# Low parts of the projection weights on VectorE in place of GpSimd, in the joined norm and projection stage of a two-block kernel

## The reference

```
for l in range(2):
    h = rmsnorm(x, mix_norm[l])                 # x: 512 x 1024
    p = h @ w_in[l]                             # w_in[l]: 1024 x IN_COLS
    qkv, z, beta_r, a_r, ... = split(p)         # qkv: 1536 columns, z: 512, beta_r and a_r: 8 each
    qkv = silu(depthwise_conv5(qkv))
    q, k, v = split(qkv)                        # 4 heads of 128 each
    q = l2norm(q) * 128 ** -0.5;  k = l2norm(k)
    beta = sigmoid(beta_r)
    g = -exp(a_log) * softplus(a_r + dt_bias)
    ... gated delta rule on q, k, v, beta, g, a second scan, the output projection, an FFN
```

## Time and profile before

| | us |
|---|---|
| median of 3 timed runs | 3571.25 (3570.12 to 3573.18) |
| the profiled execution | 3573.7 |
| its span in the trace | 3571.8 |
| POOL's busy time in the span | 320.2 |
| DVE's busy time in the span | 1649.7 |

### The profile page before, as it was taken

How to read it: one execution, slowest core, us unless ns; L and a number is a source line. 1 busy time by engine, 2 the same in 40 slices (tenths; PEclk the granted TensorE clock), 3 DMA queues, 4 the chain that set the end, 5 groups by cost and what they waited for, 6 DMA issues and landing times. The chain is left out here.

```text
span 3571.8 us, 41903 instructions
## 1 busy us (share of the span) xinstructions
PE 3124.3 (87%) x15948; PEld 2596.9 (73%) x15948; DVE 1649.7 (46%) x2194; ACT 1143.8 (32%) x1604; POOL 320.2 (9%) x228
## 2 busy tenths in 40 slices
PE   7898998987999898989998799995954689979999
PEld 5798987865887678988877588774832468758787
DVE  4566557334553365654743455333345333333233
ACT  3443643223222353354332322233102123232222
POOL 2231021001000133300200100001000000010000
PEclk9999999998999999999999899997955589989999
DMA  4101202322222310020042222223200023223222
GB/s 140 47 1 43 75 1 60 98 67 83 94 82 82 107 47 25 1 93 24 19 112 71 71 94 94 72 69 72 71 6 24 1 75 99 85 71 94 71 97 91
DMA packets 256603, 234.91 MB, mean 66 GB/s; under 512 B 22885, under 2 KB 240211, under 8 KB 255828
## 3 DMA queue, kind: packets, MB, share of 16 engines
q1 hardware_dynamic: 256468, 233.07, 21.4%
HBM read 226.75 MB, written 6.29 MB: 65 GB/s over the span
## 5 line engine op out<-in xcount | busy, mean ns | idle before, releaser
L120 PE MATMUL PS<-HHI,WHI 128*128 128x512 f32 x2080 | 825.2, 397 | 126.8 <-DVE WLO L172 112.2
L121 PE MATMUL PS<-HLO,WHI 128*128 128x512 f32 x2080 | 820.7, 395 | 0.0
L122 PE MATMUL PS<-HHI,WLO 128*128 128x512 f32 x2080 | 820.5, 394 | 0.0
L172 DVE TENSOR_TENSOR WLO<-RAW,WHI 128x1024 fp32r<-128x1024 f32 (+3 forms) x256 | 436.7, 1707 | 559.3 <-ACT WHI L168 558.2
L168 ACT CAST WHI<-RAW 128x1024 fp32r<-128x1024 f32 (+3 forms) x256 | 367.5, 1438 | 825.6 <-PE PS L122 692.0
L120 PEld LDWEIGHTS PS<-HHI,WHI 128*128 128x128 f32 x2080 | 394.7, 190 | 221.4 <-issue 82.4
L121 PEld LDWEIGHTS PS<-HLO,WHI 128*128 128x128 f32 x2080 | 394.8, 190 | 88.4 <-issue 1.0
L122 PEld LDWEIGHTS PS<-HHI,WLO 128*128 128x128 f32 x2080 | 394.2, 189 | 88.1
L120 PE MATMUL PS<-SH,WHI 128*128 128x512 f32 x800 | 317.0, 396 | 44.4 <-DVE SL L379 44.4
L121 PE MATMUL PS<-SL,WHI 128*128 128x512 f32 x800 | 315.6, 394 | 0.0
L122 PE MATMUL PS<-SH,WLO 128*128 128x512 f32 x800 | 315.2, 394 | 0.0
(11 more groups left out here) (394 smaller groups left out, 4220.5 us busy)
## 6 DMA issues: line engine op xcount, KB each, us to landing
RAW<-in_w_up SPq DMA_DIRECT2D x44, 1024.0 KB, 5.1
RAW<-in_w_in SPq DMA_DIRECT2D x68, 512.0 KB, 4.1
RAW<-in_w_in SPq DMA_DIRECT2D x27, 1024.0 KB, 5.3
RAW<-in_w_down SPq DMA_DIRECT2D x44, 512.0 KB, 3.2
RAW<-in_w_gate SPq DMA_DIRECT2D x32, 512.0 KB, 4.0
RAW<-in_w_mlp SPq DMA_DIRECT2D x16, 1024.0 KB, 5.5
RAW<-in_w_mlp SPq DMA_DIRECT2D x32, 512.0 KB, 3.2
RAW<-in_w_out SPq DMA_DIRECT2D x24, 512.0 KB, 3.4
```

What stands on the lines that cost most here:

```text
L120: e.matmul(out, wh, xh, start=first and n == 0, stop=False)
L121: e.matmul(out, wh, xl, start=False, stop=False)
L122: last = e.matmul(out, wl, xh, start=False, stop=final and n == len(quads) - 1)
L172: self.lo_st.done(dve.tensor_tensor(self.lo[:, s], self.raw[:, s], self.hi[:, s], ALU.subtract), f"unit{s}")
```

## The change

POOL's loop over tiles 4 to 15 goes. DVE gets `low(u)`, the same subtraction with the same wait for the high part, and calls it twelve times, between the convs: low(4) ahead of conv(0), low(5) behind it, low(6) behind conv(1), low(7) behind conv(2), and from conv(4) on low(i + 4) behind conv(i). The semaphore is the same under a new name. PE's, ACT's and SP's orders stay.

```diff
         def low_ready(e, u):
-            e.wait_ge(lo_dve, u + 1) if u < N else e.wait_ge(lo_pool, u - N + 1)
+            e.wait_ge(lo_dve, u + 1) if u < N else e.wait_ge(lo_late, u - N + 1)
...
+                def low(u):
+                    dve.wait_ge(hi_s, u + 1)
+                    dve.tensor_tensor(WLO[:, u % N], RAW[:, u % N], WHI[:, u % N], ALU.subtract).then_inc(lo_late, 1)
...
+                low(4)
                 conv(0)
+                low(5)
                 dve.wait_ge(S["ba_done"], 1)
                 dve.tensor_copy(BAT[0:16, :], PS[0:16, 7, :]).then_inc(S["ba_kept"], 1)
                 conv(1)
+                low(6)
                 conv(2)
+                low(7)
                 dve.wait_ge(S["ba_turned"], 1)
...
                 for i in range(3, 8):
                     conv(i)
+                    if i >= 4:
+                        low(i + 4)
                 dve.wait_ge(gate.sem, gate.place["ea"])
...
                 conv(8)
+                low(12)
...
                 conv(9)
+                low(13)
                 for n in range(4):
                     unit(n)
                 conv(10)
+                low(14)
                 for n in range(4, 8):
                     unit(n)
                 conv(11)
+                low(15)
...
             def _(pool):
                 for k in range(K):
                     pool.wait_ge(S["x_hi"], k + 1)
                     pool.tensor_tensor(pair[1][:, k, :], TK[k % 4], pair[0][:, k, :], ALU.subtract).then_inc(S["x_lo"], 1)
-                for u in range(N, T):
-                    pool.wait_ge(hi_s, u + 1)
-                    pool.tensor_tensor(WLO[:, u % N], RAW[:, u % N], WHI[:, u % N], ALU.subtract).then_inc(lo_pool, 1)
```

More of the change, by code:

```diff
@@ L427, in qkv_stage @@
     TK = [S2[:, n, :] for n in range(4)]
-    names = ("loaded0", "loaded1", "loaded2", "loaded3", "weights_hi", "weights_lo_dve", "weights_lo_pool", "tiles_done",
+    names = ("loaded0", "loaded1", "loaded2", "loaded3", "weights_hi", "weights_lo_dve", "weights_lo_late", "tiles_done",
              "wba_in", "wba_hi", "wba_lo", "eps_set", "x_squares", "x_sums", "x_root", "x_normed", "x_hi", "x_lo",
@@ L434, in qkv_stage @@
         loaded = [S[f"loaded{s}"] for s in range(N)]
-        hi_s, lo_dve, lo_pool, used = S["weights_hi"], S["weights_lo_dve"], S["weights_lo_pool"], S["tiles_done"]
+        hi_s, lo_dve, lo_late, used = S["weights_hi"], S["weights_lo_dve"], S["weights_lo_late"], S["tiles_done"]
         wl = A["w_in"][l].rearrange("(k p) n -> p k n", p=P)
```

## The result

| | before | after |
|---|---|---|
| median of 5 timed runs, us | 3573.18 (3570.12 to 3578.76) | 3600.35 (3593.70 to 3606.97) |
| the profiled execution, us | 3573.7 | 3606.97 |
| its span, us | 3571.8 | 3605.1 |
| its mean granted clock | 0.924 | 0.916 |

The change makes the kernel slower by 0.73%: the ratio is 1.0073, with a 95% interval of 1.0055 to 1.0092. That is 27 us, where 15.4 were forecast. The sign and the mechanism in the stage were right; the time lies outside the range of 3580 to 3590.5. The profiled execution of the changed kernel was the slowest of its five.

A forecast was written before the change was run, and what follows sets the result against it. PE was taken to bound the stage; per layer 5.5 us of idle plus 2.2 us of slow restart make 7.7, +15.4 us for two layers, so 3571.25 becomes 3586.6 us. The range was 3580 to 3590.5 us.

The forecast's parts named there:

- The bound and the spot: PE bounds the stage; five lows in DVE's full stretch delay Ln 0, so PE idles 5.5 us before the third sum.
- A low's price: Each subtraction moved to DVE costs 1.14 us in its queue, between 1.14 and 1.23.
- Rival D: Each low on DVE costs 1.23 us: 0.9 us more, 3587.5, inside the forecast's 76%.
- What was costed at nothing: low(4), (5) and low(11) to (15) on DVE were taken as hidden, costing PE 0.
- The slow restart: After idling before the third sum, PE restarts at the 1.2 GHz level, losing 2.2 us per layer.
- Rival A: PE idles before the third sum but its clock stays up: +11 us, 3582.3; chance 13%.
- Rival B: DVE's convs shrink without POOL's work beside them, so silu(7) stays in place: no change, 3571.3; chance 6%.
- After that nothing gives it back: Behind the third sum PE is the bound again, so its 5.5 us idle per layer is not recovered.
- two times 7.7: Both layers each lose 5.5 us of PE idle time plus 2.2 us of slow restart: +15.4 us.
- the phase of the clock is not in my hand: Remark in favour of PE's clock staying up after its idle time before the third sum; no size given.

The follow-up runs named there:

- e1: Changed kernel with low(6) to low(10) made by POOL again, the other seven lows still on DVE; 3582.84 us, ratio 1.0027.
- e2: Kernel before, all lows on POOL, plus five equal-size subtractions on DVE at the places of low(6) to low(10); 3603.35 us, ratio 1.0083.
- e11: Kernel before with 15 unused matmuls per layer added ahead of dense(15); 3583.83 us, ratio 1.0034.
- e12: Changed kernel with 15 unused matmuls per layer added ahead of dense(15); 3611.17 us, ratio 1.0101.
- e5: Changed kernel with 4 unused matmuls per layer added ahead of dense(15); 3598.66 us, ratio 1.0077.
- e8: Changed kernel with low(6) to low(10) back on POOL, plus 4 unused matmuls per layer ahead of dense(15); 3586.18 us, ratio 1.0033.
- e3: Changed kernel with dense(10) put ahead of the eight sums in PE's order; 3577.24 us, ratio 1.0009.
- e13: Changed kernel with 24 unused matmuls between the second and third sum, filling PE's wait; 3590.48 us, ratio 1.0045.
- e14: Changed kernel as it is, measured again on the same chip; 3597.18 us, ratio 1.0069.

## Why the prediction was right and wrong

**The bound and the spot: right.** PE without idle time, DVE's full stretch from the copy to BAT to conv(7), and Ln 0 ahead of the third sum as the place that decides: after the change the third sum waits 5.46 and 5.41 us, forecast 5.5. Ln 0 was forecast at 110.4 and stands at 110.85, in a stage that started 0.7 us later.

**A low's price: right,** 1.14 us in the queue. Rival D's 1.23 is out.

**What was costed at nothing: right** in the changed kernel. low(4) and (5) left 0.31 us of cover of the 0.4 that I had counted; PE idled at no place in the stage where it had not before. This cover holds only while POOL makes no lows beside it: in e1 low(5) took 2.86 us, and PE waited 1.0 us per layer.

**The slow restart: right,** 2.3 to 2.5 us by the time from the third sum to the stage's end, against 2.2. Rival A (a clock that stays up) did not happen. The Trainium skill's advice to keep elementwise work off GpSimd (GPSIMD Engine Reference, Engine selection) held for the duration of the instruction, and not for the kernel.

**Rival B: rightly small.** No conv shrank: they still take 3.80 us between lows. But the contention in it is real. The Trainium skill (GPSIMD Engine Reference, Key points) puts it at the shared SBUF interfaces, for DVE instructions with two SBUF inputs; the trace agrees in the three places looked at. The second half of the units fell from 5.03 us for four to 2.49, and in e2 a subtraction beside POOL's low took 2.12 us for 1.22; in e1 low(5) took 2.86. What the changed kernel gains by it lies under cover.

**The step that failed** is the sentence "After that nothing gives it back", and with it the sum of two times 7.7. It took for granted that what lies behind the stage costs the same when it starts later. Of the 27 us, 15 to 16 are the stage (14.8 by its windows, 15.7 by wait and restart), and the remainder, 8.4 to 11.8 with the forecast's 15.4, is for the most part the later stages at a lower granted clock: PEclk 0.94 to 0.97 in place of 0.96 to 0.99 over the four windows, which took 14.2 us more in the profiled pair. The term was missing, not mis-sized. I had noted that "the phase of the clock is not in my hand", but let it bear only on the restart in the stage.

**The range** failed with it. It allowed 1.5 us for the timing's own spread, from three runs within 3 us of each other. On the next chips the kernel before spread from 3566.9 to 3581.9, and a single program of equal code (e1) over 21 us. A term for the later stages belonged into the range on both sides, and not an even one: in single executions the four windows lay from 5 us below the profile of before (e11) to 17 above it (e12). The 0.2% named as the least that can be told from no change was thus also drawn too fine for a cause: two programs can differ by it through their start moments alone.

**Why run after run.** The clock record answers this for the second layer. Its `qkv_stage` starts at the same place against the clock in 15 of 16 profiles, so the first layer's moment does not carry over, and in both profiles of the changed kernel the delta stage behind it starts 0.1 us ahead of a fall and holds 23.9 us at 0.50. Delta and scan stage of the second layer took 5.1 us more than in the profile of before, both times.

**What stays open.** Not shown is why the second layer starts at that place, why a tenth of a us decides at some places, and why four more matmuls made e1's kernel no better. For e1, e5 and e8, one profile each is too little to say which of their runs met which clock. That extra matmuls also shift the code of PE was not tried apart; e1's spread with fixed code, along with its clock, and the equal lengths of stages that start at the same place in different programs, are the arguments against it as the main cause.

## What to carry to other kernels

Read where an engine has no idle time, and who stands behind that stretch in the next engine's queue; moved work that nobody waits for still costs its full length there, and here one exchange in PE's order (e3) took nearly all of it away. Price an idle time of PE of some 5 us at its length plus some 2.4 us for the slow restart. And where later stages keep PE busy in short pieces, expect any shift, of 1 us as of 8, to move them by several us either way: compare their windows and granted clock before blaming the change for its whole loss.

## What the runs showed of the hardware

- A stage of equal instructions took from 184.1 to 191.0 us (delta rule), or from 126.3 to 130.6 us (scan), at a mean granted clock of 0.98 to 0.94 and 0.99 to 0.95, by where its start fell against the falls of the clock. The delta stage held 6.8 us at 0.50 at the fast end and 23.9 us at the slow one.
- A kernel can gain by useless work: 24 matmuls in PE's wait made the changed kernel 6.7 us faster in its median (e13 against e14).
- A DVE subtraction of 128x1024 with two SBUF operands took 1.22 us alone, 2.12 us where it ran into one GpSimd subtraction (e2) and 2.86 us beside two (e1); both times it ended 1.1 us after the GpSimd work beside it. A DVE conv step that reads PSUM and one SBUF tensor showed no such stretch.
